# Seven slots of split weights instead of five in the feed-forwards of a two-block transformer kernel, with three loads and one addition moved

## The reference, cut to what matters

```
first block, x [256, 2048]
  h  = rmsnorm(x) * g_mix;  z = h @ w_in            # 2048 x 10248: conv parts, q, k, v, f, two gates
  x += (gc * (conv(z) @ w_conv_out) + ga * (attention(z) @ w_attn_out)) @ w_mix_out
  h  = rmsnorm(x) * g_mlp
  x += relu(h @ w_ff1)**2 @ w_ff2                   # 2048 x 8192 and 8192 x 2048
  x  = rmsnorm(x) * g_final
second block
  h  = rmsnorm(x) * attn_norm_g;  q, k, v, p = h @ w_in_2
  x += concat(attention(q, k, v, rel_bias), pool(p)) @ w_out_2
  h  = rmsnorm(x) * ffn_norm_g
  gate, val = conv3(h @ w_up) + conv_b              # 2048 x 11264
  x += (silu(gate) * val) @ w_down                  # 5632 x 2048
```

## Time and profile before

| what | us |
|---|---|
| median of 3 runs | 2383.93 |
| the 3 runs | 2383.45, 2383.93, 2384.9 |
| profiled execution | 2383.46 |
| its span (first to last instruction of the program) | 2381.6 |

### The profile page before, as it was taken

One profiled execution on the slowest core, in us unless ns is written; L12 is line 12 of the kernel. 1 busy time (PEld: TensorE's weight loads), 2 busy tenths in 40 slices (PEclk: granted clock), 3 DMA queues, 4 the chain that ended last, 5 costly groups with the idle time before them and its releaser, 6 DMA issues.

```text
span 2381.6 us, 30785 instructions
## 1 busy us (share of the span) xinstructions
PE 2376.9 (100%) x12581; PEld 2035.4 (85%) x12581; DVE 1700.7 (71%) x1804; ACT 1216.5 (51%) x1427; POOL 0.2 (0%) x4
## 2 busy tenths in 40 slices
PE   9999999999999999999999999999999999999999
PEld 8888888888888888888888888888888888888887
DVE  6565666666568868868768667855778778886788
ACT  5444454554545445445445555555555455545554
POOL 0000000000000000000000000000000000000000
PEclk9999999999999999999999999999999999999999
DMA  7566556666555665655665565555655665566655
GB/s 253 160 187 196 167 185 196 191 188 196 186 187 178 219 216 189 213 181 198 202 190 193 182 185 160 171 183 186 186 181 194 196 192 176 186 219 186 188 173 181
DMA packets 238040, 452.15 MB, mean 190 GB/s; under 512 B 16569, under 2 KB 20779, under 8 KB 237771
## 3 DMA queue, kind: packets, MB, share of 16 engines
q1 hardware_dynamic: 237147, 449.07, 59.3%
q10 hardware_dynamic: 752, 1.12, 0.1%
HBM read 446.46 MB, written 3.67 MB: 189 GB/s over the span
## 4 chain that ended last, share of the span: by engine, by line
PE 97%; DVE 2%; ACT 0%; issue 0%; ACTq 0%; DVEq 0%
PE PS L684 41%; PE PS L686 21%; PE PS L717 11%; PE PS L718 11%; PE PS L719 11%; DVE WL L1279 1%; PE PS L648 0%; PE PS L615 0%; PE PS L636 0%; PE PS L657 0%; ACT WH L840 0%; PE PS L542 0%; PE PS L625 0%; DVE PB L1259 0%; PE PS L553 0%
## 5 line engine op out<-in xcount | busy, mean ns | idle before, releaser
L1279 DVE TENSOR_TENSOR WL<-RAW,WH 128x1024 fp32r<-128x1024 f32 (+1 forms) x844 | 1002.0, 1204 | 520.6 <-ACT WH L840 519.1
L684 PE MATMUL PS<-XHL,WH 128*128 128x512 f32 x3968 | 1248.9, 396 | 0.0
L840 ACT ACTIVATE WH<-RAW 128x1024 fp32r<-128x1024 f32 (+1 forms) x845 | 867.5, 1041 | 744.4 <-PE PS L686 478.3
L686 PEld LDWEIGHTS PS<-XHL,WL 128*128 128x128 f32 x3968 | 745.4, 188 | 176.0
L686 PE MATMUL PS<-XHL,WL 128*128 128x256 f32 x3968 | 779.7, 278 | 0.0
L684 PEld LDWEIGHTS PS<-XHL,WH 128*128 128x128 f32 x3968 | 605.1, 189 | 2.1 <-issue 1.0
L717 PE MATMUL PS<-WH,MHL 128*128 128x512 f32 x1000 | 390.2, 390 | 0.0
L719 PE MATMUL PS<-WH,MHL 128*128 128x512 f32 x1000 | 389.2, 389 | 0.0
L718 PE MATMUL PS<-WL,MHL 128*128 128x512 f32 x1000 | 389.1, 389 | 0.0
L719 PEld LDWEIGHTS PS<-WH,MHL 128*128 128x128 f32 x1000 | 187.7, 188 | 39.3
L717 PEld LDWEIGHTS PS<-WH,MHL 128*128 128x128 f32 x1000 | 187.7, 188 | 38.8 <-issue 0.3
(11 more groups left out here) (212 smaller groups left out, 1374.6 us busy)
## 6 DMA issues: line engine op xcount, KB each, us to landing
RAW<-in_w_ff SPq DMA_DIRECT2D x256, 512.0 KB, 4.1
RAW<-in_w_in SPq DMA_DIRECT2D x224, 512.0 KB, 3.9
RAW<-in_w_up SPq DMA_DIRECT2D x176, 512.0 KB, 4.1
RAW<-in_w_down SPq DMA_DIRECT2D x88, 512.0 KB, 4.4
RAW<-in_w_mix_out SPq DMA_DIRECT2D x32, 512.0 KB, 4.0
RAW<-in_w_out SPq DMA_DIRECT2D x32, 512.0 KB, 3.7
RAW<-in_w_conv_out SPq DMA_DIRECT2D x16, 512.0 KB, 3.7
RAW<-in_w_attn_out SPq DMA_DIRECT2D x16, 512.0 KB, 4.3
```

Source lines behind the costliest of these rows:

```text
L684: mm(PS[:, b + p.banks[j], :], h[:, k, j * P:(j + 1) * P], x[:, kc, :], start=st, stop=False)
L686: t = mm(PS[:, b + p.banks[j], 0:T], l[:, k, j * P:(j + 1) * P], x[:, kc, 0:T], start=False, stop=en)
L840: act(high, raw, AF.Copy).then_inc(*own.made(hi, i))
L1279: tt(low, raw, high.bitcast(f32), sub).then_inc(*own.made(lo, i))
```

## The change

What it does:

- WHX and WLX are two more slots each, behind five. They lie where V2 and BIAS lie. They are in use from ff(0,0) to the entry ahead of ff2(3,2), and from gate 0 to the end; in between, and before, there are five slots. So there are seven in both feed-forwards.
- Each entry has its slot and the entry that had it before (`prior`) from a list; `ahead_of` lets both engines split ahead as far as the slots are free by the plan: six entries with seven slots, four with five. In the order of the two engines' work, the split of entry n + 6 stands where that of n + 4 stood.
- AS moves to the unused end of PB. AXH and AXL get a third part that nothing uses. GF moves over the last quarter of XHL, and its load is issued after ff(3,3), the last user of XHL there, at the load five units behind the unit of the entry eight behind ff(3,3).
- The load of BIAS is issued when the two more slots are given back, in ff2(3,2). The addition of the mask (line 1848) moves from ahead of ff(3,1) to ahead of K0.

The diff, cut to its core:

```
+NX = 2
-    ahead: int = AHEAD
+    ahead: int = NS + NX
...
+        with ExitStack() as c:
+            sb("Xpad", [P, 12 * 2 * T], c=c)
+            GF = sb("GF", [P, D], c=c)
...
-            AXH = sb("AXH", [P, 2, 4, P], f32r, c=c)
-            AXL = sb("AXL", [P, 2, 4, P], f32r, c=c)
-            AS = sb("AS", [P, 4, P], c=c)
+            AXH = sb("AXH", [P, 3, 4, P], f32r, c=c)
+            AXL = sb("AXL", [P, 3, 4, P], f32r, c=c)
             EV = sb("EV", [P, 2, 512], c=c)
-            sb("QK2pad", [P, 4096 - 1536 - 2048], c=c)
-            GF = sb("GF", [P, D], c=c)
+            WHX = sb("WHX", [P, NX, UNIT], f32r, c=c)
+            WLX = sb("WLX", [P, NX, UNIT], f32r, c=c)
...
+        AS = PB[:].rearrange("p a b -> p (a b)")[:, 1024:1536].rearrange("p (a b) -> p a b", a=4)
...
+        more = {item_of["ff", 0, 0].parts[0].ent: branches_end, item_of["gate", 0].parts[0].ent: item_of["wo", 0].end}
+        fewer = (item_of["ff2", 3, 2].parts[0].ent,)
+        turns, slot, prior = [(n, None) for n in range(NS)], [], []
+        for n in range(len(ents)):
+            if n in more:
+                turns = [(NS + i, more[n]) for i in range(NX)] + turns
+            if n in fewer:
+                turns = [t for t in turns if t[0] < NS]
+            place, before = turns.pop(0)
+            slot.append(place)
+            prior.append(before)
+            turns.append((place, n))
+        more_used = max(n for n in range(fewer[0]) if slot[n] >= NS)
+
+        def ahead_of(n, most):
+            last = n
+            while last + 1 < len(ents) and last < n + most and (prior[last + 1] is None or prior[last + 1] < n):
+                last += 1
+            return last
...
-        BIAS_AFTER = ents[item_of["ff", 1, 0].parts[0].ent][1] + AHEAD - 1 + NR
+        GF_AFTER, BIAS_AFTER = (ents[n + NS + NX + 1][1] + NR for n in (x_end, more_used))
...
+                if i == GF_AFTER:
+                    own.wait_ge(*used[x_end])
+                    e.dma_start(GF[:], io["g_final"].rearrange("(a n) -> a n", a=1).to_broadcast([P, D])
+                                ).then_inc(s_gf, 16)
                 if i == BIAS_AFTER:
                     own.wait_ge(s_er, er_all)
-                    own.wait_ge(*used[branches_end])
+                    own.wait_ge(*used[more_used])
...
-                    if i >= NS:
-                        own.wait_ge(*used[i - NS])
+                    if prior[i] is not None:
+                        own.wait_ge(*used[prior[i]])
...
-                    split_to(p.ent + it.ahead)
+                    split_to(ahead_of(p.ent, it.ahead))
...
-                            split_to(ent + AHEAD)
+                            split_to(ahead_of(ent, NS + NX))
...
-                elif it.key == ("ff", 3, 1):
+                elif it.key == ("K", 0):
                     chain()
                     own.wait_ge(s_wp, 16)
                     tt(BIAS[:], BIAS[:], over4(M, 8), add).then_inc(*own.made())
```

More of the change, by code:

```diff
@@ L202, in first_half @@
             self.put("proj", ("q", half), self.wide(w1, 0, ALLK, C0["q"] + 512 * half), ("X", "mix"), args=h,
-                     mid=mid if half == 0 else {}, ahead=1 if half == 0 else AHEAD)
+                     mid=mid if half == 0 else {}, ahead=1 if half == 0 else NS + NX)
             self.put("proj", ("k", half), self.wide(w1, 0, ALLK, C0["k"] + 512 * half), ("X", "mix"), args=h,
@@ L406, in build, with high_slot, low_slot @@
         units, ents, items = plan.units, plan.ents, plan.items
+        item_of = {it.key: it for it in items}
+        branches_end = item_of["attn", 3].end
+        more = {item_of["ff", 0, 0].parts[0].ent: branches_end, item_of["gate", 0].parts[0].ent: item_of["wo", 0].end}
[16 more added lines that the diff above has]
+            return last
+        def high_slot(n):
+            return WH[:, slot[n]] if slot[n] < NS else WHX[:, slot[n] - NS]
+        def low_slot(n):
+            return WL[:, slot[n]] if slot[n] < NS else WLX[:, slot[n] - NS]
         def landed(u):
@@ L413, in raw_view, with wviews @@
             return RAW[:, u % NR, 0:per * n].rearrange("p (k n) -> p k n", k=per)
-        def wview(buf, e):
+        def wviews(e):
             what, u = ents[e]
             _, per, n = units[u] if what != "b22" else (None, 1, 512)
-            return buf[:, e % NS, 0:per * n].rearrange("p (k n) -> p k n", k=per)
+            return [b[:, 0:per * n].rearrange("p (k n) -> p k n", k=per) for b in (high_slot(e), low_slot(e))]
         def paired(e):
-            return WH[:, e % NS, 0:NKC * 16].rearrange("p (k n) -> p k n", k=NKC)
+            return high_slot(e)[:, 0:NKC * 16].rearrange("p (k n) -> p k n", k=NKC)
         def pieces(e):
@@ L426, in pieces @@
             n = units[u][1] * units[u][2]
-            raw, high, low = RAW[:, u % NR, 0:n], WH[:, e % NS, 0:n], WL[:, e % NS, 0:n]
+            raw, high, low = RAW[:, u % NR, 0:n], high_slot(e)[:, 0:n], low_slot(e)[:, 0:n]
             if units[u][2] == 8:
@@ L485, in build @@
         rel_all, er_all = 48, 16 * 16
-        item_of = {it.key: it for it in items}
-        BIAS_AFTER = ents[item_of["ff", 1, 0].parts[0].ent][1] + AHEAD - 1 + NR
-        branches_end = item_of["attn", 3].end
+        x_end = item_of["ff", 3, 3].end
+        GF_AFTER, BIAS_AFTER = (ents[n + NS + NX + 1][1] + NR for n in (x_end, more_used))
         def out_rows(tb, g, half):
@@ L513, in sync @@
                     del waiting[:3]
+                if i == GF_AFTER:
+                    own.wait_ge(*used[x_end])
+                    e.dma_start(GF[:], io["g_final"].rearrange("(a n) -> a n", a=1).to_broadcast([P, D])
+                                ).then_inc(s_gf, 16)
                 if i == BIAS_AFTER:
                     own.wait_ge(s_er, er_all)
-                    own.wait_ge(*used[branches_end])
+                    own.wait_ge(*used[more_used])
                     e.dma_start(BIAS[:], bass.AP(ERD.tensor, ERD.offset + P - 1, [[8 * 384 - 1, P], [384, 8], [1, T]])
                                 ).then_inc(s_wp, 16)
-                    e.dma_start(GF[:], io["g_final"].rearrange("(a n) -> a n", a=1).to_broadcast([P, D])
-                                ).then_inc(s_gf, 16)
             for g in range(2):
@@ L676, in features @@
                     own.wait_ge(*lo[p.ent])
-                    h, l = wview(WH, p.ent), wview(WL, p.ent)
+                    h, l = wviews(p.ent)
                     for k, kc in enumerate(p.kcs):
@@ L731, in group @@
                             own.wait_ge(*lo[ent])
-                            h, l = wview(WH, ent), wview(WL, ent)
+                            h, l = wviews(ent)
                             order = [(k, tb) for k in range(2) for tb in range(2)]
@@ L1215, in scalar @@
                     split_to(it.end)
-                    split_to(it.end + AHEAD)
+                    split_to(ahead_of(it.end, AHEAD))
                 elif it.steps:
```

## The result

The changed kernel takes **2389.8 us** (median of 10 runs, 2388.6 to 2391.95), the kernel before, run beside it, 2384.82 (10 runs, 2383.45 to 2385.44): ratio **1.0022**, 95% interval 1.0013 to 1.0032, or 3.1 to 7.6 us more. Forecast were 2385.4 and a range up to 2388.4, so the time lies above the range. The profiled execution took 2391.44 us, its span is 2389.6 us, 8.0 more than before. 1.35 us of that lie in the first 10 us (PE waits for the load of g_mix, 1.30 us between two starts instead of 0.35, and its small matmuls behind that take longer).

A forecast was written before the change was run, and what follows sets the result against it. PE, busy 2376.9 of 2381.6 us, was taken as the bound. Profiled 2383.46 - 0.8 (stalls) + 2.3 (addition) = 2385.0; from the runs' median, 2383.93 + 1.5 = 2385.4 us, range 2382.8 to 2388.4.

The forecast's parts named there:

- What bounds it: Whole kernel: PE is busy nearly throughout, idle 4.7 us in all; the slots can win only 0.8 us.
- the two stalls: PE's waits for a weight split in down(1,0) and down(2,0); both were to go, -0.8 us.
- The addition ahead of K0: Mask addition delays the `fold` that PE needs at `spread` after K0's second part: +2.3 us, paid once.
- The clock: Rival, chance 0.06: PE's stop ahead of K0 lowers the clock, 2.5 us more, 2387.9 us.
- `sevens`: Last step of `sevens`, needed at next group's start, gets no later; 0.44 and 0.46 us in hand; no cost.
- a rival for the stalls: Rival, chance 0.08: stalls stay, say because ScalarE's splits wait for loads of RAW, still five places; 2386.2 us.
- `sevens` is pushed back: Rival, chance 0.06: two more splits delay `sevens`, stalling down(1,1) and down(2,1) by 2.0 + 1.9 us; 2389.3 us.
- Loads, switching, addresses: GF and BIAS loads, slot switches at ff(0,0) and gate 0, and moved buffers: hidden or unchanged, nothing.

The follow-up runs named there:

- e4: Changed kernel with the mask addition ahead of Q1 and, behind a group's last seven-product pair, pending work ahead of further splits: 2382.63 us, ratio 0.9996.
- e1: Kernel before with only the mask addition moved ahead of K0, five slots and all loads as before: 2387.39 us, ratio 1.0014.
- e3: Changed kernel with pending work (`sevens`) ahead of further splits behind a group's last seven-product pair, on ScalarE and VectorE: 2386.46 us, ratio 1.0013.
- e2: Changed kernel with the mask addition one item later, ahead of Q1 instead of K0: 2385.7 us, ratio 1.0009.
- e7: Kernel before with the mask addition in halves, one ahead of ff(3,1), one ahead of K0: 2385.9 us, ratio 1.0009.
- e9: Changed kernel with the mask addition ahead of Q1 and groups of ff2 and down splitting only four entries ahead: 2382.76 us, ratio 1.0000.
- e8: Kernel before plus two addition-sized instructions ahead of K0 that leave BIAS as it is: 2390.58 us, ratio 1.0029.
- e5: Kernel before with RAW given four places instead of five: 2394.77 us, ratio 1.0044.
- e6: Changed kernel with the mask addition ahead of Q1 and RAW given four places instead of five: 2399.96 us, ratio 1.0069.

## Why the prediction was wrong

The median came out 4.4 us above the one forecast. Point by point:

- **What bounds it: right.** PE with its waits is still the whole story, and what the slots could win was -0.8. e4, with both new losses away, measures -0.81, and its profile has no wait for a split in the feed-forwards (one of 0.5 us stands at 8.81 us, at the start of the program). By the starts the two stalls were 0.41 and 0.46 us, 0.9 in all. Three readings on the way were loose. VectorE didn't have "next to no rest" between 2053.89 and the late split: it idled 1.01, 1.26 and 0.53 us there, each time for ScalarE. The 1.56 us ahead of 2053.89 are a wait for ScalarE by the row, and for a free slot only through it. And no weight load takes 1.1 us: that is the sum of PEld's two waits, while a load starts 0.22 us ahead of its matmul (2080.20 and 2080.42).
- **The addition ahead of K0: right in place, size and cause.** Predicted 2.3, between the starts 2.33 more than before, and e1's runs at full clock are 2.5 above.
- **The clock: wrong, as a chance.** "So far PE has never stood for 2.3 us once running" was true, and I read it as reason for 0.06 where it was a reason to know nothing. The clock is 0.999 in 9 of 10 runs of the changed kernel, 9 of 11 of e1, 10 of 11 of e3. Its price was 2.5 "between"; it is 1.3 (e3's two kinds of runs), 1.5 (e1's) or 1.6 (the starts in the traces), at or below the lower of my bounds, 1.6.
- **`sevens`: this step failed.** The sentence was: "Between the idle place and this step VectorE does as many splits as before (18 ...), so the step doesn't get later". I put its cost at nothing; it is 3.4 us in the trace and 3.1 by e2 less e4. The count holds (18 in the profile after too), but it counts VectorE's work where the step hangs on ScalarE's queue as well, and there on landings. I had named the five places of RAW, but as a rival for the stalls, not for this step. And I checked the slack at two starts (0.44, 0.46 us) and not at the one where it broke first: 1847 us, with 1.2 us in hand and 2.6 us of delay. Slack alone didn't say where the delay would come. The rival "`sevens` is pushed back" had the wait right, with 2.0 + 1.9 us at two starts; it was 1.5, 0.6 and 0.8 at three, by another cause.
- **Loads, switching, addresses: right**, nothing.

The two unforeseen parts by experiment: `sevens` is e2 less e4, 2385.7 - 2382.63 = 3.1 us; stop with clock is e3 less e4, 3.8 us, of which 2.3 were foreseen. Against the kernel before beside them that gives -0.8 + 3.8 + 3.1 = 6.1 us. The traces give -0.9 + 2.3 + 1.6 + 3.4 + 0.2 (the `fold` at 1564) = 6.6, and 8.0 less the late start of 1.35 is 6.6 too. The measured 5.0 (3.1 to 7.6) is lower, but it stands against a kernel before of 2384.82, of whose ten runs eight were above 2384.6, in the upper group that e7 speaks of; against its later medians of 2383.3 to 2383.45 it would be 6.4. How well the experiments' 6.1 fits is in part luck, for e2's median holds runs up to 2387.5 that no profile explains.

The range already held the fall of the clock (2387.9 and 0.5 of scatter). It had no room for `sevens`: 2385.4 + 1.6 + 3.1 = 2390.1, where 2389.8 was measured.

## What to carry over

More buffers at the end of a chain move the wait to its next link: with seven slots behind five landing places, an engine that works in order meets the loads instead of the slots, and what is queued behind it pays. Where a change lets an engine run further ahead, list what due work stands behind the added instructions, on every engine of the chain, and give that work its turn first (e4) or limit the lead (e9). And when a change makes TensorE stop for two microseconds in the midst of dense work, price the clock as likely, with somewhat under half of the stretch that runs slow (1.6 of 3.4 us here), and look for it in a window, since the mean of the page hides it.

## What the runs showed of the hardware

I hadn't expected a stop this short to move the clock. Behind the stop at K0 (2.21 us in the profiles of the changed kernel, e1 and e3) the clock fell to 1.2 GHz in 9 of 10, 9 of 11 and 10 of 11 runs by their mean clocks, for 3.41 us in the two of these profiles that have the fall, and cost 1.3 to 1.6 us. After 1.14 us (e7) it fell in none of 11. With 4.53 us (e8) it fell during the stop and was at half for 6.83 us in the profile. From start to start these three gaps are 2.49, 1.43 and 4.82 us. In e5's profiled execution a gap of 2.43 us between two starts was followed by a fall and one of 1.85 was not; in e6's, gaps of 3.58, 2.81 and 4.02 were and one of 1.65 was not, nor was the one of 1.77 at 1847 us in the changed kernel. That the same stop of 2.21 us has it in one execution and not in the next (e1) was seen; what decides it was not looked into.
